# Expert weights of a mixture-of-experts block loaded in transfers of 1 MB on twelve semaphores instead of 2 MB on six

## The chip, the cores and the metric

The kernel runs on one core of a Trainium2 chip. A core has five engines with instruction queues of their own: TensorE (PE, matrix products), VectorE (DVE), ScalarE (ACT), GpSimd (POOL) and SyncE (SP), which here issues most transfers. 16 DMA engines move data between the chip's main memory and the core's on-chip memory of 128 partitions. Engines wait for each other, and for transfers, through semaphores. The metric is the time on the device in microseconds (us); lower is better.

## The reference, cut to what matters

A decoder block: two attention mixers in parallel, then a mixture of experts with 4 of 32 experts for each of 512 tokens, all in float32. The change touches only the expert stage:

```python
D_MODEL = 1024; SEQ = 512; N_EXPERTS = 32; TOP_K = 4; D_FF = D_MODEL
def moe(h, router_w, router_b, w1, b1, w2, b2):
    logits = (xt @ router_w + router_b).astype(jnp.float32)
    top_v, top_i = lax.top_k(logits, TOP_K)
    gate = jax.nn.softmax(top_v, axis=-1)
    ...
    def expert_block(args):
        xb, e = args
        hc = xb @ w1[e] + b1[e]          # w1[e]: 1024 x 2048, 8 MB
        gt = jnp.minimum(hc[:, :D_FF], SWIGLU_LIMIT)
        up = jnp.clip(hc[:, D_FF:], -SWIGLU_LIMIT, SWIGLU_LIMIT)
        glu = gt * jax.nn.sigmoid(SWIGLU_ALPHA * gt)
        return ((up + 1.0) * glu) @ w2[e] + b2[e]   # w2[e]: 1024 x 1024, 4 MB
    ...
```

Each expert has 12 MB of weights, 384 MB in all, and every byte is loaded once.

## The kernel before

**Stages.** Until about 440 us the kernel normalises, projects and runs both attention mixers. From there to about 520 us it forms the output projection, routes the tokens and stores what the experts need. From about 521 us it works through the 32 experts, and at the end it adds up and normalises the rows.

**An expert.** `expert(e, b)` on TensorE (L1729) runs the first product of expert e, `up` (L1670), and then the second product of expert e−1, `second` (L1781), which calls `down` (L1699). `up` takes eight slabs of the first matrix, c = 0 to 7, each 128 partitions of 2048 floats (1 MB), and runs 12 matmuls of 32 x 512 on each (three groups of 32 tokens, four column blocks); the profile counts two records for each of these float32 matmuls, so 24 a slab and 192 an expert. `down` does likewise with four slabs s of the second matrix. Expert 0 is different: `first_expert` (L1745) runs `up` in two rounds, two token groups and then the third, and only the second round reports its slabs as used.

**The ring.** `ring` (L165) holds 12 slabs of 1 MB as six places of two (`pair_slot`, `slab`, L445 and L449). Places 0 and 1 take the second matrix (`W2_SLOTS`), places 4, 5, 2, 3 the first (`W1_LATER`); expert 0 uses places 0 and 1 and four other buffers (`FIRST_SLABS`, L465), loaded by `load_lone` (L672) in single slabs. So all 12 MB of an expert's turn are under way or in use at once.

**Loading.** SyncE issues all of it, in program order. `load_pair(e, u)` (L661) issues one transfer of 2 MB, u = 0 to 3 from the first matrix and 4, 5 from the second; a partition's share is 4096 neighbouring floats. `load_w1(e)` (L713) waits until `w1_used` says that TensorE is through with both slabs of a place, then issues the pair; `load_w2` (L718) does the same with `w2_used`. TensorE counts these up after each slab (`used`). `load_last_w2` (L723) loads expert 31's second matrix into places of the first, in single slabs already, but waits for both slabs of a place. TensorE waits for a pair on `slabs_loaded[u]` ahead of its first slab (L1742, L1788). Each place has a semaphore of its own, since a transfer counts 16 on its semaphore, engine by engine.

**Beside it.** GpSimd gathers each expert's token rows with three indirect transfers (L910) and adds each expert's result into main memory with two (L930, L923), on another queue of the same 16 DMA engines.

Of the kernel before, what the change touches and what calls it, by code (L numbers as in the profile page):

```python
# [146 lines left out]
def hybrid_block(nc, x, positions, norm1_g, w_in, cmp_pos_emb, cmp_w1, cmp_w2, fox_f_bias, w_proj_nsa,  # L147
                 w_proj_fox, w_out, norm2_g, router_w, router_b, expert_w1, expert_b1, expert_w2,
                 expert_b2, norm_f_g, rope_freqs, out):
    with ExitStack() as ctx:  # L150
# [3 lines left out]
        def sem(name):  # L154
            return ctx.enter_context(nc.semaphore(name))
# [294 lines left out]

            return pair_slot(k)[:, 2048 * h:2048 * h + 2048]

        def last_load(s):

            return (last_loaded if s % 2 else slabs_loaded)[s // 2], 16

        def slabs_of(slots):

            return [slab(k, h) for k in slots for h in range(2)]
# [38 lines left out]
        consts2 = sem("consts2")  # L498
        table_stored, last_table_stored = sem("table_stored"), sem("last_table_stored")
        idx_ready = sem("idx_ready")  # L500
        slabs_loaded = [sem("slabs_loaded%d" % b) for b in range(6)]
        w1_used = sem("w1_used")
        w2_used = sem("w2_used")
        now_ready = sem("now_ready")
# [7 lines left out]
        gt_ready = sem("gt_ready")  # L512
        hc_free = sem("hc_free")
        third_root, third_normed = sem("third_root"), sem("third_normed")
        last_loaded = [sem(f"last_loaded{u}") for u in range(2)]
        sg_ready = sem("sg_ready")
        act_ready = sem("act_ready")
        gT_ready = sem("gT_ready")
# [24 lines left out]
        def _(sp):  # L543
# [114 lines left out]
            sp.dma_start(g2k, norm2_g[0].rearrange("(p c) -> p c", p=P)).then_inc(router_loaded, 16)  # L658
            sp.dma_start(r_bias, router_b[0:1, :].partition_broadcast(P)).then_inc(router_loaded, 16)

            def load_pair(e, u):  # L661

                if u < NK // 2:
                    src = expert_w1[0].rearrange("e (p u c) n -> e p u (c n)", p=P, c=2)
                else:
                    src = expert_w2[0].rearrange("e (p u c) n -> e p u (c n)", p=P, c=4)
                at = u % (NK // 2)
                slot = (W1_FIRST if isinstance(e, int) and e == 0 else W1_LATER)[u] if u < NK // 2 else W2_SLOTS[at]
                src = src[bass.ds(e, 1), :, at, :] if not isinstance(e, int) else src[e:e + 1, :, at, :]
                sp.dma_start(pair_slot(slot), src.rearrange("e p n -> (e p) n")).then_inc(slabs_loaded[u], 16)  # L670

            def load_lone(c):  # L672
                src = expert_w1[0].rearrange("e (p c) n -> e p c n", p=P)[0, :, c, :]
# [32 lines left out]
            store_table(EARLY)  # L706
            store_x2(EARLY)
            load_pair(1, 1)
            for u in range(2):
                sp.wait_ge(w1_used, 2 * u + 2)  # L710
                load_pair(0, NK // 2 + u)

            def load_w1(e):  # L713
                for u in range(NK // 2):
                    sp.wait_ge(w1_used, NK * (e - 1) + 2 * u + 2)
                    load_pair(e, u)

            def load_w2(e):  # L718
                for u in range(2):
                    sp.wait_ge(w2_used, 4 * (e - 1) + 2 * u + 2)  # L720
                    load_pair(e, NK // 2 + u)

            def load_last_w2():  # L723
                for s in range(NK // 2):
                    src = expert_w2[0].rearrange("e (p s c) n -> e p s (c n)", p=P, c=2)[E - 1:E, :, s, :]
                    sp.wait_ge(w1_used, NK * (E - 1) + s // 2 * 2 + 2)
                    sp.dma_start(slab(W2_LAST[s // 2], s % 2), src.rearrange("e p n -> (e p) n")).then_inc(*last_load(s))

            load_w1(2)
            load_w2(1)  # L730
# [519 lines left out]
        def _(pe):  # L1250
# [478 lines left out]
            def expert(e, b):  # L1729

                if isinstance(e, int) and e == 1:
                    pe.wait_ge(rows_ready, 1)
                else:
                    pe.wait_ge(hc_free, e)
                def used(c, ins):
                    ins.then_inc(w1_used, 1)
                    if isinstance(e, int) and e == 1 and c == NK // 2:
                        spread_rows(SLOTS_AT, 0, 2 * E, row_of.rearrange("p v e -> p (v e)")).then_inc(table_full, 1)

                pe.wait_ge(xT_ready, e + 2)  # L1740
                up(b, slabs_of(W1_LATER),
                   lambda c: pe.wait_ge(slabs_loaded[c // 2], 16 * e + (16 if c < LONE else 0)) if c % 2 == 0 else None, used)  # L1742
                second(e - 1, 1 - b)

            def first_expert():  # L1745
# [22 lines left out]
                def first_loaded(c):  # L1768
                    if c >= LONE:
                        loaded, value = lone_loaded[c - LONE]  # L1770
                        pe.wait_ge(loaded, value + 16)
                    elif c % 2 == 0:
                        pe.wait_ge(slabs_loaded[c // 2], 16)

                pe.wait_ge(xT_ready, 1)
                up(0, FIRST_SLABS, first_loaded, between,
# [4 lines left out]
            def second(e, b):  # L1781

                pe.wait_ge(gT_ready, e + 1)
                if not (isinstance(e, int) and e == 0):
                    pe.wait_ge(y_ready, e)
                else:
                    pe.wait_ge(idx_ready, 8)
                down(b, W2_SLOTS, lambda s: pe.wait_ge(slabs_loaded[(NK + s) // 2], 16 * e + 16) if s % 2 == 0 else None,  # L1788
                     lambda s, ins: ins.then_inc(w2_used, 1))

            def second_last(b):

                pe.wait_ge(b_last_ready, 2)
                for n, w in enumerate((512, 256)):
                    pe.matmul(ps[:, Y_LAST + n, 0:w], ident[:, :], b_last[n], start=True, stop=False, skip_group_check=True)
                pe.wait_ge(gT_ready, E)
                down_last(b, W2_LAST, lambda s: pe.wait_ge(last_load(s)[0], 16 if s % 2 else 16 * E + 16), lambda s, ins: ins.then_inc(w2_used, 1))

            first_expert()
            expert(1, 1)  # L1800
# [706 lines left out]
```

## Time and profile before

| | us |
|---|---|
| median of 3 runs | 1561.2 (1560.4 to 1562.38) |
| profiled execution | 1560.53 |
| its span | 1558.8 |
| TensorE busy in it | 1513.6 (97%) |
| mean share of the DMA engines' time used by SyncE's queue | 71.2% |
| moved | 463.85 MB |

The span runs from the first to the last instruction of the profiled execution. A busy TensorE is a TensorE with a matmul under way, not one at its peak. TensorE ran at the full granted clock of 2.4 GHz (1.00) throughout the expert loop. In the rows, "DMA share" is the mean busy share of the 16 DMA engines; it can pass 1 where packets overlap. The time of a transfer is given from its issue on SyncE to its landing.

### The profile page before, as it was taken

To read this page: it belongs to the slowest core of one execution; us is meant where nothing else is said; L and a number is where in the kernel's file an instruction comes from. 1 tells how busy PE (TensorE), PEld (TensorE's weight loads), DVE (VectorE), ACT (ScalarE), POOL (GpSimd) and SP (SyncE) were. 2 spreads that over 40 slices of the span, in tenths; PEclk is the share of its full clock that TensorE was granted. 3 is DMA by queue.
4 is the path that set the end of the run, shared out by engine and by line. 5 is a ranking of instruction groups with operands and counts; after the bars stand their busy time and mean duration, and the time that the engine had idled before them with its cause. 6 is when DMAs were issued, how large, how long until landed. Compare 5 with 4: busy or idle time off the path is not lost.

```text
span 1558.8 us, 30600 instructions
## 1 busy us (share of the span) xinstructions
PE 1513.6 (97%) x12626; PEld 625.6 (40%) x12627; DVE 595.9 (38%) x1114; ACT 219.0 (14%) x468; POOL 299.5 (19%) x381
## 2 busy tenths in 40 slices
PE   7999999999999999999999999999999999999993
PEld 4654555666445433333333333333333333333331
DVE  4104555333225562244224433433343334433342
ACT  4212444323212100000000000000000000000001
POOL 2000001533000202122212221222122212121101
PEclk9999999999999999999999999999999999999997
DMA  9122130531273499999999999999999999999984
GB/s 241 28 55 54 41 81 14 167 93 27 71 290 129 172 388 403 415 417 419 414 414 419 419 413 419 417 418 412 419 419 417 411 416 418 415 418 409 412 365 135
DMA packets 109595, 463.85 MB, mean 298 GB/s; under 512 B 33698, under 2 KB 72562, under 8 KB 84464
## 3 DMA queue, kind: packets, MB, share of 16 engines
q1 hardware_dynamic: 95680, 446.42, 71.2%
q0 software_dynamic: 13872, 16.83, 4.7%
q8 instruction: 30, 0.49, 0.1%
q14 instruction: 13, 0.11, 0.0%
HBM read 452.94 MB, written 18.89 MB: 303 GB/s over the span
## 4 chain that ended last, share of the span: by engine, by line
PE 74%; DMA 21%; issue 2%; ACT 1%; DVE 1%; ACTq 0%; DVEq 0%; SPq 0%; PEld 0%; PEldq 0%; POOLq 0%
PE ps L1676 30%; DMA ring<-in_expert_w 20%; PE ps L1260 12%; PE ps L1685 9%; PE ps L1410 7%; PE ps L1694 4%; PE ps L1634 4%; PE ps L1395 2%; PE ps L1372 2%; PE ps L1382 2%; ACT mixT L1091 1%; PE ps L1550 0%; DMA xs<-in_x 0%; PE ps L1586 0%; DMA oT_nsa<-table,v_win 0%
## 5 line engine op out<-in xcount | busy, mean ns | idle before, releaser
L1676 PE MATMUL ps<-ring,oT_fox 128*32 128x512 f32 x6048 | 658.7, 593 | 4.5 <-DMA ring<-in_expert_w 4.0
L1676 PEld LDWEIGHTS ps<-ring,oT_fox 128*32 128x32 f32 x6048 | 194.8, 110 | 447.6 <-issue 410.4
L2332 DVE TENSOR_TENSOR mixT<-ps,mask 128x768 f32<-128x768 f32 x64 | 61.0, 953 | 577.1 <-PE ps L1676 577.1
L1685 PE MATMUL ps<-ring,hT 128*32 128x512 f32 x2048 | 267.8, 592 | 1.5 <-DMA ring<-in_expert_w 1.3
L1694 PE MATMUL ps<-ring,hT 128*32 128x256 f32 x2048 | 158.6, 379 | 0.0
L1410 PE MATMUL ps<-hT,ring 128*128 128x512 f32 x304 | 137.0, 597 | 0.0
L1694 PEld LDWEIGHTS ps<-ring,hT 128*32 128x32 f32 x2048 | 69.3, 110 | 150.0 <-issue 149.9
L910 POOL DMA_INDIRECT oT_nsa<-table,pc x93 | 105.3, 1132 | 47.1 <-POOL pc L905 27.7
L1190 ACT ACTIVATE mixT<-mixT 128x768 f32<-128x768 f32 x32 | 27.0, 844 | 614.6 <-DVE mixT L2336 614.6
L1260 PE MATMUL ps<-hT,ring 128*128 128x512 f32 x208 | 92.1, 603 | 0.2 <-ACT hT L1021 0.2
L1685 PEld LDWEIGHTS ps<-ring,hT 128*32 128x32 f32 x2048 | 68.2, 110 | 59.0 <-issue 17.8
L905 POOL COPY pc<-pc 128x3 int32 (+1 forms) x31 | 7.3, 234 | 406.4 <-DMA x<-hT,v_win 386.1
L1410 PEld LDWEIGHTS ps<-hT,ring 128*128 128x128 f32 x304 | 55.4, 190 | 64.0 <-issue 64.0
L1200 ACT ACTIVATE hT<-rope_pT,v_fox 128x512 f32<-128x512 f32 (+1 forms) x62 | 34.7, 607 | 311.0 <-DVE rope_pT L2368 311.0
L918 POOL COPY v_win<-v_win 128x1 int32 (+1 forms) x64 | 9.7, 178 | 270.8 <-ACT hT L1200 255.1
L930 POOL DMA_INDIRECT x<-hT,v_win x32 | 52.1, 1627 | 43.5 <-POOL v_win L918 25.5
L1091 ACT ACTIVATE mixT<-ps,st 128x128 f32<-128x128 f32 (+1 forms) x96 | 49.1, 535 | 78.5 <-DVE st L1967 78.5
L1260 PEld LDWEIGHTS ps<-hT,ring 128*128 128x128 f32 x208 | 39.7, 193 | 49.0 <-issue 48.8
L1634 PE MATMUL ps<-ring,mixT 128*128 128x512 f32 x128 | 59.4, 602 | 0.0
L2321 DVE STREAM_TRANSPOSE oT_fox<-oT_nsa 128x768 f32<-128x768 f32 x31 | 49.6, 1600 | 7.1 <-DVE mixT L2340 7.1
L923 POOL DMA_INDIRECT x<-hT,v_win x32 | 50.3, 1571 | 9.8 <-issue 9.8
L2328 DVE STREAM_TRANSPOSE hT<-mixT 128x768 f32<-128x768 f32 x32 | 51.2, 1600 | 1.1
(309 smaller groups left out, 1131.7 us busy)
## 6 DMA issues: line engine op xcount, KB each, us to landing
ring<-in_expert_w SPq DMA_DIRECT2D x188, 2048.0 KB, 23.3
ring<-in_w_in SPq DMA_DIRECT2D x28, 512.0 KB, 4.8
ring<-in_w_out SPq DMA_DIRECT2D x8, 512.0 KB, 9.1
ring<-in_expert_w SPq DMA_DIRECT2D x4, 1024.0 KB, 23.6
ring<-in_w_in SPq DMA_DIRECT2D x1, 2144.0 KB, 13.3
xs<-in_x SPq DMA_DIRECT2D x4, 512.0 KB, 5.1
ring<-in_w_in SPq DMA_DIRECT2D x8, 256.0 KB, 3.6
ring<-in_w_proj_nsa SPq DMA_DIRECT2D x16, 128.0 KB, 2.8
```

The source lines that it names most:

```text
L910: pool.indirect_dma_start(out=xg_rows[b][:, 256 * g:256 * g + 256], out_offset=None, in_=table_quarter, in_offset=bass.IndirectOffsetOnAxi ...
L923: pool.indirect_dma_start(out=x2_quarter, out_offset=bass.IndirectOffsetOnAxis(ap=now_quarter[b], axis=0), in_=yb[b][:, 512:768], in_offse ...
L930: pool.indirect_dma_start(out=x2_half, out_offset=bass.IndirectOffsetOnAxis(ap=now_half[b], axis=0), in_=yb[b][:, 0:512], in_offset=None, ...
L1091: last = act.activation(probs[:, h, P_OFF[t]:P_OFF[t] + P * (t + 1)], scores(h, t), ACT.Exp, bias=ngm[:, h, t:t + 1], accum_out=sums[:, h, ...
L1260: last = pe.matmul(dst, lhs(c), rhs(c), start=(c == 0), stop=(c == n - 1))
L1410: ins = pe.matmul(w, w_c(c), hT[:, c, :], start=(c == 0), stop=(c == NK - 1))
L1634: ins = pe.matmul(ps[:, u, :], mix_t[:, t, k, :], w_o[k][:, n * 512:(n + 1) * 512], start=(k == 0), stop=(k == NK - 1))
L1676: ins = pe.matmul(wide(ps[TG * j:TG * j + TG, hc + g, :]), xT[b][:, g, c, :], up_slab(slabs[c], j), start=(c == 0), stop=(c == NK - 1), ti ...
L1685: ins = pe.matmul(ps[TG * q:TG * q + TG, bank, :], gT[b][:, q // 2, c, :], rows[:, at:at + 512], start=(c == 0 and bank == Y_BANK), stop=( ...
L1694: ins = pe.matmul(ps[TG * q:TG * q + TG, bank, 0:256], gT[b][:, 2, c, :], rows[:, at:at + 256], start=(c == 0 and bank == Y_BANK + 1), sto ...
L2328: return dve.transpose(gT[b], act_b.rearrange("p g (m c) -> p g c m", c=NK))
L2332: return dve.tensor_tensor(to, half, b_up[:, 256 * n:256 * n + 256].unsqueeze(1).broadcast_to([P, NG, 256]), ALU.add)
```

## The change

Every transfer of expert weights becomes one slab of 1 MB. `load_slab(e, c)` replaces the body of `load_pair`; a partition's share is now 2048 neighbouring floats. In the loop SyncE waits for one used slab ahead of each transfer. Twelve semaphores take the place of six, and of `last_loaded`; four of them (for the second matrix) are older ones used again, which start from a value that is not zero. TensorE waits ahead of each slab, except in expert 0, where it waits for two slabs ahead of every second one.

```diff
-        slabs_loaded = [sem("slabs_loaded%d" % b) for b in range(6)]
+        slabs_loaded = [(sem("slabs_loaded%d" % c), 0) for c in range(8)]
+        slabs_loaded += [(w_gate_loaded[0], 160), (w_gate_loaded[1], 96), (w_mix_loaded[0], 192), (w_mix_loaded[1], 192)]
...
+            def load_slab(e, c):
+
+                if c < NK:
+                    src = expert_w1[0].rearrange("e (p c) n -> e p c n", p=P)
+                    slabs = slabs_of(W1_LATER) if not (isinstance(e, int) and e == 0) else FIRST_SLABS
+                else:
+                    src = expert_w2[0].rearrange("e (p s c) n -> e p s (c n)", p=P, c=2)
+                    slabs = slabs_of(W2_SLOTS)
+                src = src[bass.ds(e, 1), :, c % NK, :] if not isinstance(e, int) else src[e:e + 1, :, c % NK, :]
+                sp.dma_start(slabs[c % NK], src.rearrange("e p n -> (e p) n")).then_inc(slabs_loaded[c][0], 16)
+
             def load_pair(e, u):
-
-                if u < NK // 2:
-                    src = expert_w1[0].rearrange("e (p u c) n -> e p u (c n)", p=P, c=2)
...
-                sp.dma_start(pair_slot(slot), src.rearrange("e p n -> (e p) n")).then_inc(slabs_loaded[u], 16)
+                for c in (2 * u, 2 * u + 1):
+                    load_slab(e, c)
...
-            for u in range(2):
-                sp.wait_ge(w1_used, 2 * u + 2)
-                load_pair(0, NK // 2 + u)
+            for s in range(4):
+                sp.wait_ge(w1_used, s + 1)
+                load_slab(0, NK + s)
...
             def load_w1(e):
-                for u in range(NK // 2):
-                    sp.wait_ge(w1_used, NK * (e - 1) + 2 * u + 2)
-                    load_pair(e, u)
+                for c in range(NK):
+                    sp.wait_ge(w1_used, NK * (e - 1) + c + 1)
+                    load_slab(e, c)
...
-                    sp.wait_ge(w1_used, NK * (E - 1) + s // 2 * 2 + 2)
-                    sp.dma_start(slab(W2_LAST[s // 2], s % 2), src.rearrange("e p n -> (e p) n")).then_inc(*last_load(s))
+                    sp.wait_ge(w1_used, NK * (E - 1) + s + 1)
+                    sp.dma_start(slab(W2_LAST[s // 2], s % 2), src.rearrange("e p n -> (e p) n")).then_inc(slabs_loaded[s][0], 16)
...
-                   lambda c: pe.wait_ge(slabs_loaded[c // 2], 16 * e + (16 if c < LONE else 0)) if c % 2 == 0 else None, used)
+                   lambda c: pe.wait_ge(slabs_loaded[c][0], 16 * e + (16 if c < LONE else 0)), used)
...
-                down(b, W2_SLOTS, lambda s: pe.wait_ge(slabs_loaded[(NK + s) // 2], 16 * e + 16) if s % 2 == 0 else None,
+                down(b, W2_SLOTS, lambda s: pe.wait_ge(slabs_loaded[NK + s][0], 16 * e + (slabs_loaded[NK + s][1] + 16)),
```

`load_w2` changes as `load_w1` does, and so do the waits of `second_last` and of `first_loaded`.

On SyncE, at the entry to the expert loop (from expert 0's second matrix on), before:

```order
L670 DMA ring<-in_expert_w 128x4096 [waits w1_used] x6
L670 DMA ring<-in_expert_w 128x4096 [waits w2_used] x2
L731 UNCONDITIONAL_BRANCH
L731 ISA
L670 ISA [waits w1_used]
L670 DMA ring<-in_expert_w 128x4096
L715 REGISTER_ALU
```

and now:

```order
L666 DMA ring<-in_expert_w 128x2048 [waits w1_used] x12
L666 DMA ring<-in_expert_w 128x2048 [waits w2_used] x4
L731 UNCONDITIONAL_BRANCH
L731 ISA
L666 ISA [waits w1_used]
L666 DMA ring<-in_expert_w 128x2048
L715 REGISTER_ALU
```

Twice as many transfers of half the size, each behind a wait of its own; nothing else changed its place.

On TensorE, at the end of the first product and the start of the second in the loop, before:

```order
L1676 MATMUL ps<-ring,oT_fox 32x512 [waits slabs_loaded3]
L1676 MATMUL ps<-ring,oT_fox 32x512 x23
L1785 REGISTER_ALU [waits gT_ready]
L1788 ISA [waits y_ready]
L1685 MATMUL ps<-ring,hT 32x512 [waits slabs_loaded4]
L1685 MATMUL ps<-ring,hT 32x512 x3
L1694 MATMUL ps<-ring,hT 32x256 x4
```

and now:

```order
L1676 MATMUL ps<-ring,oT_fox 32x512 [waits slabs_loaded6]
L1676 MATMUL ps<-ring,oT_fox 32x512 x11
L1676 MATMUL ps<-ring,oT_fox 32x512 [waits slabs_loaded7]
L1676 MATMUL ps<-ring,oT_fox 32x512 x11
L1786 REGISTER_ALU [waits gT_ready]
L1789 ISA [waits y_ready]
L1685 MATMUL ps<-ring,hT 32x512 [waits w_gate_loaded0]
L1685 MATMUL ps<-ring,hT 32x512 x3
L1694 MATMUL ps<-ring,hT 32x256 x4
```

The matmuls keep their order; a wait now stands ahead of every 12 of them instead of every 24, and in the second product a register step comes with some of the new waits.

## Rows read from the trace of the kernel before

**Rows 1.** The page: TensorE and DMA engines, busy tenths in 40 slices.
```profile
PE   7999999999999999999999999999999999999993
...
DMA  9122130531273499999999999999999999999984
```

**Rows 2.** The chain that ended last, in order of time: start us, us, what.
```profile
1014.27 20.60 PE ps L1676 x192
1045.19 20.64 PE ps L1676 x192
1065.99 25.69 DMA ring<-in_expert_w
1091.72 5.40 PE ps L1676 x48
...
1474.63 5.36 PE ps L1676 x48
1490.31 20.60 PE ps L1676 x192
```

**Rows 3.** Waits of TensorE's weight loads, 1045 to 1490 us: total, times, longest.
```profile
PEld ps L1676 <- DMA ring<-in_expert_w: 33.2, 51, 1.4
```

**Rows 4.** Transfers issued 612 to 643, then 1091 to 1123 us: KB, us to landing.
```profile
ring<-in_expert_w SPq DMA_DIRECT2D x6, 2048.0 KB, 12.5
...
ring<-in_expert_w SPq DMA_DIRECT2D x6, 2048.0 KB, 25.9
```

**Rows 5.** Timeline of TensorE and of SyncE's issues around 541 and 555 us.
```profile
541.16 1.90 PE L1676 MATMUL ps<-ring,oT_fox 128*32 128x512 f32 x16
542.88 0.50 PE L1661 MATMUL ps<-v_fox,ident 96*32 96x28 f32 x24
...
543.12 2.36 SPq L670 DMA_DIRECT2D ring<-in_expert_w  x2
...
555.46 0.33 SPq L670 DMA_DIRECT2D ring<-in_expert_w  x1
```

**Rows 6.** Busy time by window; the last two columns are DMA share and GB/s.
```profile
540.00:545.00 5.00, 5.00 (x76) 1.71 (x69) 3.19 (x11) 0.00 (x0) 3.28 (x5) 1.00 0.32 60
...
555.00:560.00 5.00, 5.00 (x52) 1.50 (x48) 4.62 (x11) 0.84 (x1) 0.00 (x0) 1.00 0.75 275
560.00:565.00 5.00, 5.00 (x68) 1.71 (x64) 4.67 (x9) 0.00 (x0) 0.00 (x0) 1.00 1.04 413
```

**Rows 7.** DMA queues, 700 to 1000 us: packets, MB, share of 16 engines; issues.
```profile
q1 hardware_dynamic: 8230, 119.84, 94.3%
q0 software_dynamic: 4211, 5.09, 7.1%
...
ring<-in_expert_w SPq DMA_DIRECT2D x59, 2048.0 KB, 19.3
```

**Rows 8.** DMA, 1484 to 1492 us, 16 KB packets.
```profile
DMA packets 240, 3.51 MB, mean 438 GB/s; under 512 B 26, under 2 KB 26, under 8 KB 26
...
q1 hardware_dynamic: 240, 3.51, 102.4%
```

**Rows 9.** DMA, 493 to 496 us, 8 KB packets.
```profile
q1 hardware_dynamic: 171, 1.27, 101.0%
```

**Rows 10.** DMA, 297 to 303 us, 4 KB packets.
```profile
DMA packets 684, 2.49 MB, mean 415 GB/s; under 512 B 77, under 2 KB 77, under 8 KB 683
...
q1 hardware_dynamic: 683, 2.48, 102.1%
```

**Rows 11.** Three issues: start on SyncE, and us to landing.
```profile
441.08 0.43 SPq L670 DMA_DIRECT2D ring<-in_expert_w  x1
...
ring<-in_expert_w SPq DMA_DIRECT2D x1, 2048.0 KB, 8.4
...
442.03 0.43 SPq L674 DMA_DIRECT2D rope_pT<-in_expert_w  x1
...
rope_pT<-in_expert_w SPq DMA_DIRECT2D x1, 1024.0 KB, 12.5
...
443.28 0.59 SPq L670 DMA_DIRECT2D ring<-in_expert_w  x1
...
ring<-in_expert_w SPq DMA_DIRECT2D x1, 2048.0 KB, 21.0
```

**Rows 12.** Lines 1788 and 670: ns min/median/max, first and last start.
```profile
L1788 PEldq FUSED_REGOPS  x14: 37/37/37, 630.3 to 1445.4; - x14
...
L670 SPq DMA_DIRECT2D ring<-in_expert_w x188: 327/333/785, 441.1 to 1490.5; - x188
```

**Rows 13.** The chain of 530 to 562 us: the first expert's second gather.
```profile
533.94 4.44 DMA oT_nsa<-table,v_win
```

More of the change, by code:

```diff
@@ L451, in slab @@
             return pair_slot(k)[:, 2048 * h:2048 * h + 2048]
-        def last_load(s):
-            return (last_loaded if s % 2 else slabs_loaded)[s // 2], 16
         def slabs_of(slots):
@@ L514, in hybrid_block @@
         third_root, third_normed = sem("third_root"), sem("third_normed")
-        last_loaded = [sem(f"last_loaded{u}") for u in range(2)]
         sg_ready = sem("sg_ready")
@@ L659, in _ @@
             sp.dma_start(r_bias, router_b[0:1, :].partition_broadcast(P)).then_inc(router_loaded, 16)
-            def load_pair(e, u):
-                if u < NK // 2:
-                    src = expert_w1[0].rearrange("e (p u c) n -> e p u (c n)", p=P, c=2)
[L665 to L669, printed above, removed]
-                sp.dma_start(pair_slot(slot), src.rearrange("e p n -> (e p) n")).then_inc(slabs_loaded[u], 16)
+            def load_slab(e, c):
[7 more added lines that the diff above has]
+                sp.dma_start(slabs[c % NK], src.rearrange("e p n -> (e p) n")).then_inc(slabs_loaded[c][0], 16)
+            def load_pair(e, u):
+                for c in (2 * u, 2 * u + 1):
+                    load_slab(e, c)
             def load_lone(c):
@@ L708, in _ @@
             load_pair(1, 1)
-            for u in range(2):
-                sp.wait_ge(w1_used, 2 * u + 2)
-                load_pair(0, NK // 2 + u)
+            for s in range(4):
+                sp.wait_ge(w1_used, s + 1)
+                load_slab(0, NK + s)
             def load_w1(e):
-                for u in range(NK // 2):
-                    sp.wait_ge(w1_used, NK * (e - 1) + 2 * u + 2)
-                    load_pair(e, u)
+                for c in range(NK):
+                    sp.wait_ge(w1_used, NK * (e - 1) + c + 1)
+                    load_slab(e, c)
             def load_w2(e):
-                for u in range(2):
-                    sp.wait_ge(w2_used, 4 * (e - 1) + 2 * u + 2)
-                    load_pair(e, NK // 2 + u)
+                for s in range(4):
+                    sp.wait_ge(w2_used, 4 * (e - 1) + s + 1)
+                    load_slab(e, NK + s)
             def load_last_w2():
@@ L1772, in first_loaded @@
                     elif c % 2 == 0:
-                        pe.wait_ge(slabs_loaded[c // 2], 16)
+                        for n in range(2):
+                            pe.wait_ge(slabs_loaded[c + n][0], 16)
                 pe.wait_ge(xT_ready, 1)
@@ L1796, in second_last @@
                 pe.wait_ge(gT_ready, E)
-                down_last(b, W2_LAST, lambda s: pe.wait_ge(last_load(s)[0], 16 if s % 2 else 16 * E + 16), lambda s, ins: ins.then_inc(w2_used, 1))
+                down_last(b, W2_LAST, lambda s: pe.wait_ge(slabs_loaded[s][0], 16 * E + 16), lambda s, ins: ins.then_inc(w2_used, 1))
             first_expert()
```

## The prediction, made before the changed kernel was run

> **What bounds the kernel now.** I read the page by slices first. TensorE is busy almost everywhere, but from the fifteenth slice on the 16 DMA engines are at 9 tenths or more as well [rows 1]. So two resources are full in the expert loop, and the question is which wait ends last. The chain of the work that ended last answers it: until 1045 us an expert's 192 matmuls of the first product follow each other every 30.92 us (1014.27 to 1045.19) with no transfer in the chain; from 1065 us on the chain steps through a weight transfer in nearly every expert [rows 2]. The waits say the same: from 1045 to 1490 us TensorE's weight loads waited 51 times for a transfer of expert weights, 33.2 us in all, which contains 0.3 us each of ordinary spacing [rows 3].
>
> Two periods follow. TensorE alone needs 30.92 us per expert. The transfers need (1474.63 − 1091.72) / 12 = 31.91 us [rows 2], 0.99 us more. Up to 1045 us the difference is paid from the lead of the ring: a transfer lands 12.5 us after its issue in one early expert, 25.9 us after it in a late one [rows 4]. From 1045.19 to 1490.31 us lie 14 experts, 445.12 us, where 14 x 30.92 = 432.88 would do: TensorE loses 12.2 us to transfers. That is all that faster weights could return. The queue never runs dry there, so **issuing a transfer earlier in the middle of the loop brings nothing**. The last binding landing, at 1474.63 us (the fourth pair of expert 30's first matrix), is fixed by when the continuous stretch of DMA work begins and by how much engine time that work takes.
>
> **The change part by part.** *The start of the stretch.* The second matrix of expert 0 is asked for at 543.12 us, when two slabs are used; the 16 matmuls of the first two slabs run from 541.16 us for 1.9 us [rows 5]. The new wait is for one slab, so the request comes one half of 1.72 us earlier (16 matmuls to the next at 542.88), **−0.86 us**. The DMA engines are at 0.32 in that slice [rows 6], so nothing is in the way. The next place comes free at 555.46 us [rows 5]; the engines were at 0.75 between 555 and 560 us and full (1.04) in the slice after it [rows 6]. A half place comes free 2.58 us before (24 matmuls at 0.107 us, a quarter of 20.60 / 2 [rows 2]), while the work before it still runs, so that hole of 0.25 x 5 closes: **−1.25 us**.
>
> *The landing.* Before, TensorE starts a pair when both of its slabs are there. Now it starts the first when that one is there and needs the second 2.58 us later. After the last binding landing one slab, not two, is left of the pair: **−2.58 us**. All three gains together are −4.7 us. With weights of 1 MB the last slabs (expert 31's second matrix) are asked for one slab earlier, which nobody waits for.
>
> *The packets.* A pair row is 4096 floats (16 KB) per partition, a slab row 2048 (8 KB). Each engine moves a slab in eight packets of 8 KB, and moved its share in four of 16 KB. From the first transfer of the stretch to the binding one lie 4 (w2 of expert 0) + 29 x 8 (w1 of 2 to 30) + 28 x 4 (w2 of 1 to 28) = 348 slabs, hence 348 x 4 = **1392 added packets per engine**. What one costs beside its bytes is the decisive unknown. All sizes below include one completion packet to eight data packets, before as after, so nothing more is owed for the doubled completions.
> - 16 KB, in the loop: 8230 packets, 16 x 57 of them completions (59 issues, 119.84 MB is 7314 rows), took 94.3% of 16 x 300 us: 619 ns a row [rows 7]. With hardly any other traffic, 3.51 MB (214 rows) in 102.4% of 16 x 8 us: 612 ns [rows 8].
> - 8 KB: 1.27 MB (155 rows) in 101.0% of 16 x 3 us: 313 ns, or 626 ns for 16 KB [rows 9]. Against 619 and 612 that is **6.7 to 13.1 ns** for the added packet.
> - 4 KB (the output projection's weights): 2.48 MB (606 rows) in 102.1% of 16 x 6 us: 161.7 ns, 647 ns for 16 KB in four packets; three added ones cost 28 to 34.6 ns, **9.4 to 11.5 ns** each [rows 10].
> - By landings, farther off: the one pair lands at 441.08 + 8.4 = 449.5, two 8 KB transfers later it is 442.03 + 12.5 = 454.5, two pairs later 443.28 + 21.0 = 464.3 us [rows 11]. That is 5.05 us against 4.88 for 2 MB: 0.17 us over eight added packets, 21 ns, with an uncertainty of about as much since landings are given to 0.1 us.
>
> The lower end is zero: an engine that reads the next row while it writes the last may show no cost of its own. I see no reason for one below zero. I take 10 ns, where the 4 KB rows stand, which have most packets: 1392 x 10 ns = **+13.9 us**. 6.7 ns gives +9.3, 13.1 gives +18.2.
>
> The Trainium skill ("DMA: Bandwidth & Descriptors", section "Why small descriptors are slow (HBM only)") puts about 3 cycles on each packet, and its section "Where 436 GB/s comes from" gives the fabric 850 MHz; an estimate from these is 3.5 ns, so +4.9 us in place of +13.9, and no change in the sum. The rows of 4 KB packets speak for about three times that.
>
> *Instructions.* TensorE's sequencer gets two or three more register steps per expert in the second product, 37 ns each where such steps stand now [rows 12]. Now they stand between the products, and the pass still takes 30.92 us, so they hide behind queued matmuls. Uncovered, three per expert would be 0.11 us, less than the 0.99 us by which transfers are the longer, so even then nothing. SyncE issues 12 transfers per expert and not 6, about 0.33 us each [rows 12]: 4 us of 31. *Expert 0's second gather* (4.44 us on the chain [rows 13]) shares engines with long packets; shorter ones could bring it forward by a few tenths, counted at nothing.
>
> Sum: 13.9 − 4.7 = +9.2 us. The profiled execution took 1560.5 us (span 1558.8 and 1.7 around it), 0.7 below the median of 1561.2: **1570.4 us** on the median.
>
> **The rivals.** *Overhead overlaps.* An added packet costs nothing because the next row's read is under way, and only the three gains are left: 1561.2 − 4.7 = **1556.5 us**, faster. It decides from 3.4 ns (4.7 / 1392) down. For it: packets overlap in the records, whose shares exceed 100% [rows 8, 10]. Against: shares exceed it for 4 KB packets too, and these move 415 GB/s where the 16 KB ones move 438 in their window. *A small overhead*, 1.2 to 5.6 ns, leaves the sum within 3.1 us of nothing; at 3.5 ns it is 1561.2 + 0.2 = **1561.4 us**. This is the result the section on small descriptors would give, and the rows lie above it. *A cost per transfer*, not per packet, as the landings would have it at 21 ns per packet: 28.7 − 4.7 gives **1585 us**; the windows of packets, which are finer, speak against it. That the lead is not gained (the binding wait moves on to expert 30's second matrix) would change the sum by under 2.6 us and lies inside the range.
>
> **How the numbers follow.** The likeliest case, 5.7 to 13 ns, holds 0.68 and gives 1564.5 to 1575. Small overhead 0.14, overlap 0.13, cost per transfer 0.05. A measurement of this kernel tells about 0.2%, 3.1 us, from no change. Slower is 0.68 + 0.05 less what of the first could still measure as the same: 0.71; same 0.16; faster 0.13. The range goes from 1556 (all overlapped) to 1577, which takes in 13.1 ns and some 2 us more; what it leaves out is most of the cost-per-transfer case and the tails, under 0.2.
>
> **What would show it.** Right, if the period of binding landings late in the loop is about 31.91 + 48 x 0.010 = 32.4 us, an 8 KB packet in the loop takes half of 629 ns, the first wait of TensorE for a transfer comes earlier than 1065 us, and the request for expert 0's second matrix starts near 542.3. The three gains are right if the hole at 555 to 560 us is gone and waits end with one slab of 24 matmuls before the next landing. I am wrong if the period stays at 31.9 us, which means no cost per packet; or if gathers and scatters, now served between shorter packets, take less engine time than the 7.1% they have [rows 7], which I counted as unchanged.

## The result and the profile after

| | before | after |
|---|---|---|
| median | 1560.8 (1559.86 to 1562.38, 6 runs) | 1569.82 (1568.09 to 1572.27, 6 runs) |
| span of the profiled execution | 1558.8 | 1566.3 |
| ratio | | 1.0055 [1.0045, 1.0065] |

The change makes the kernel slower by 9.0 us, where 9.2 was forecast. Both kernels' slices look alike at first, and that is the first reading: nothing new stands still, the same resource is full for longer. The page after, TensorE's and the DMA engines' busy tenths in 40 slices (they answer [rows 1]), then queue q1 over the whole span (packets, MB, share of 16 engines):

```profile
PE   7999999999999999999999999999999999999993
...
DMA  9122130521283599999999999999999999999994
...
q1 hardware_dynamic: 122752, 446.43, 72.0%
```

The chain of work that ended last, of after (start, duration, what; it answers [rows 2]):

```profile
982.75 20.60 PE ps L1676 x192
1013.67 12.87 PE ps L1676 x120
1026.58 2.78 PE ps L1676 x24
1029.40 5.87 PE ps L1676 x48
1035.43 29.00 DMA ring<-in_expert_w
...
1485.18 28.03 DMA ring<-in_expert_w
1513.26 5.41 PE ps L1676 x48
```

Until 1013.67 us TensorE keeps its 30.92 us per expert, as before. The first wait for weights comes inside that expert, at 1026.6 us, and not behind 1045.19: the ring's lead is used up one expert sooner. The last piece is new too. Before, the last binding landing was at 1474.63 us in expert 30 and TensorE ran at its own pace from there. Now it is the landing at 1513.26 us, in expert 31's first matrix, with two slabs (48 matmuls) left.

**The start of the stretch.** Timeline of after (start, us; [rows 5] is the same place before):

```profile
540.29 1.90 PE L1676 MATMUL ps<-ring,oT_fox 128*32 128x512 f32 x16
...
541.39 1.19 SPq L666 DMA_DIRECT2D ring<-in_expert_w  x2
```

The request starts 1.10 us after the 16 matmuls do, and started 1.96 us after them: 0.86 us earlier, the first term of the sum. The matmuls themselves also start 0.87 us earlier (540.29 against 541.16). That isn't the change's doing: SyncE's first issue into the ring is already 0.9 us earlier (440.2 us, [rows 12] has 441.1), and the granted clock of the first 100 us was 1.00 in this execution and 0.98 in the one of before. Then the windows of after (TensorE, weight loads, DVE, ACT, POOL busy; granted clock; DMA share; GB/s; before in [rows 6]):

```profile
540.00:545.00 5.00, 5.00 (x72) 1.55 (x60) 1.44 (x7) 0.00 (x0) 3.54 (x5) 1.00 0.58 196
545.00:550.00 5.00, 4.85 (x69) 2.68 (x69) 3.50 (x9) 0.00 (x0) 0.22 (x1) 1.00 1.01 402
550.00:555.00 5.00, 5.00 (x52) 1.45 (x48) 4.66 (x11) 0.00 (x0) 0.00 (x0) 1.00 0.96 375
555.00:560.00 5.00, 5.00 (x52) 1.56 (x48) 4.65 (x10) 0.84 (x1) 0.00 (x0) 1.00 1.05 357
```

From 555 to 560 us the DMA engines are full (1.05) where they were at 0.75. The hole is closed.

**In the loop.** DMA, 700 to 1000 us, of after ([rows 7] before):

```profile
DMA packets 20440, 123.18 MB, mean 411 GB/s; under 512 B 4097, under 2 KB 4241, under 8 KB 5999
...
q1 hardware_dynamic: 16244, 118.31, 95.0%
q0 software_dynamic: 4196, 4.88, 7.0%
...
x<-hT,v_win POOLq DMA_INDIRECT x20, 9.4
```

118.31 MB are 14442 rows of 8192 bytes, which took 95.0% of 16 x 300 us: 315.8 ns each, 631.5 for 16 KB where one 16 KB row took 619. The added packet costs 12.6 ns by the rows. Queue q0, GpSimd's gathers and scatters, keeps its share (7.0%, before 7.1%), but a scatter lands 9.4 us after its issue instead of 13.1.

TensorE's waits of 900 to 1500 us, after (us in all, times, longest):

```profile
PEld ps L1676 <- DMA ring<-in_expert_w: 61.0, 106, 1.5
PEld ps L1685 <- DMA ring<-in_expert_w: 26.2, 52, 1.1
```

Before, the first of these rows had 51 waits in the same stretch, the numbers of [rows 3]. There are twice as many now and they are a little shorter, 0.58 us each instead of 0.65, since TensorE goes on at each slab.

### The profile page after: what moved, and what is told of

It is laid out like the page before. It is cut to its first block, busy times and chain, and to the rows that moved or that the text cites. A ratio compares the mean times of both kernels' runs of the same rounds, so it can differ in the third digit from the quotient of the medians.

```text
span 1566.3 us, 31381 instructions
## 1 busy us (share of the span) xinstructions
PE 1517.4 (97%) x12626; PEld 616.5 (39%) x12627; DVE 594.7 (38%) x1114; ACT 219.1 (14%) x468; POOL 290.7 (19%) x381
## 4 chain that ended last, share of the span: by engine, by line
PE 70%; DMA 19%; SPq 5%; issue 2%; DVE 1%; ACT 1%; ACTq 0%; DVEq 0%; PEld 0%; PEldq 0%; POOLq 0%
PE ps L1676 27%; DMA ring<-in_expert_w 18%; PE ps L1260 12%; PE ps L1685 9%; PE ps L1410 7%; SPq L666 5%; PE ps L1694 4%; PE ps L1634 4%; PE ps L1395 2%; PE ps L1372 2%; PE ps L1382 2%; ACT mixT L1091 1%; PE ps L1550 0%; DMA xs<-in_x 0%; PE ps L1586 0%
## 5 line engine op out<-in xcount | busy, mean ns | idle before, releaser
L1694 PEld LDWEIGHTS ps<-ring,hT 128*32 128x32 f32 x2048 | 66.6, 110 | 152.7 <-issue 152.6
L910 POOL DMA_INDIRECT oT_nsa<-table,pc x93 | 97.2, 1045 | 47.1 <-POOL pc L905 26.9
L1685 PEld LDWEIGHTS ps<-ring,hT 128*32 128x32 f32 x2048 | 63.5, 110 | 69.8 <-DMA ring<-in_expert_w 26.2
## 6 DMA issues: line engine op xcount, KB each, us to landing
ring<-in_w_in SPq DMA_DIRECT2D x1, 2144.0 KB, 13.1
```

The lines of the kernel that those rows point to most:

```text
L910: pool.indirect_dma_start(out=xg_rows[b][:, 256 * g:256 * g + 256], out_offset=None, in_=table_quarter, in_offset=bass.IndirectOffsetOnAxi ...
L1685: ins = pe.matmul(ps[TG * q:TG * q + TG, bank, :], gT[b][:, q // 2, c, :], rows[:, at:at + 512], start=(c == 0 and bank == Y_BANK), stop=( ...
L1694: ins = pe.matmul(ps[TG * q:TG * q + TG, bank, 0:256], gT[b][:, 2, c, :], rows[:, at:at + 256], start=(c == 0 and bank == Y_BANK + 1), sto ...
```

## The experiments

Three theories stood against each other. **Per packet**: each added packet costs its engine some 10 ns, and the half-sized release and wait give back 4.7 us. **Per transfer**: it is the doubled number of transfers that costs. **Small overhead**: packets cost next to nothing. Ratios are against the kernel before on the same chip.

### Halves alone

Transfers of 1 MB, but released and awaited in pairs as before. Against after:

```diff
                 for c in range(NK):
-                    sp.wait_ge(w1_used, NK * (e - 1) + c + 1)
+                    if c % 2 == 0:
+                        sp.wait_ge(w1_used, NK * (e - 1) + c + 2)
                     load_slab(e, c)
...
-                   lambda c: pe.wait_ge(slabs_loaded[c][0], 16 * e + (16 if c < LONE else 0)), used)
+                   lambda c: [pe.wait_ge(slabs_loaded[c + n][0], 16 * e + (16 if c < LONE else 0)) for n in range(2)] if c % 2 == 0 else None, used)
```

The second matrix likewise.

> Transfers of 1 MB in pairs: both slabs of a place are asked for together once both are used, and TensorE waits for both ahead of the first. So this has the smaller transfers without the earlier release and without the wait per slab. If 1392 added packets at 10 ns each cost 13.9 us and the two kinds of finer waiting gave back 4.7 us in the changed kernel, this is 1560.8 + 13.9 = about 1575 us, ratio to before 1.009. Rival: the finer waits give nothing, and the packets cost only what was measured for the whole, 9 us: then this is 1570 us, ratio 1.0058, as the changed kernel is.

Measured: 1575.37 us against 1560.44, ratio 1.0095 [1.0078, 1.0112]. 14.9 us over 1392 added packets per engine are 10.7 ns each. The hole is back, in the windows of this kernel (columns as above), here with the matmuls of the first two slabs, the first request behind them (SyncE's timeline, 538 to 580 us), and the last landing that TensorE waited for, from the chain:

```profile
540.00:545.00 5.00, 4.25 (x24) 1.74 (x28) 2.16 (x10) 0.00 (x0) 3.38 (x5) 0.67 0.17 47
555.00:560.00 5.00, 5.00 (x52) 1.47 (x48) 4.72 (x9) 0.00 (x0) 0.00 (x0) 1.00 0.72 297
...
545.13 1.89 PE L1679 MATMUL ps<-ring,oT_fox 128*32 128x512 f32 x16
...
547.09 28.84 SPq L666 DMA_DIRECT2D ring<-in_expert_w  x12
...
1522.86 5.36 PE ps L1679 x48
```

The stretch begins 4.0 us later here than before (547.09 against 543.12), so the hole does too: it lies between 558 and 562 us, with DMA shares of 0.54, 0.06, 0.79 and 0.79 in slices of one us. This profiled execution is the slowest of its kernel (1577.67 us). TensorE stood idle for 1.1 us around 540 us, waiting for a gather, and then had a granted clock of 0.50, the lower level (1.2 GHz), from 542 to 545 us. The two executions above show 1.00 there. How early an execution reaches the stretch varies, from 539 to 545 us for these matmuls over the profiles of this document, and that is in every end-to-end number below.

So the change is a cost of about 15 us and a gain of about 6 (1.0095 against 1.0055 is 6.2 us, the medians' differences 14.9 and 9.0 give 5.9; forecast 4.7). The traces, with the different starts taken out, give the 4.7 us that were forecast: expert 31's first product ends at 1522.86 + 5.36 = 1528.22 us here and at 1513.26 + 5.41 = 1518.67 us in after, 9.55 us apart, and 4.84 of these are the start (545.13 against 540.29).

### 2 MB in rows of 8 KB

Before, with the number of transfers left alone: one transfer of 2 MB whose two slabs are not neighbours in main memory, so a partition gets two rows of 8 KB. TensorE takes the slabs in the order 0, 4, 1, 5 and so on.

```diff
+                    slot, rows = (W1_FIRST if first else W1_LATER)[u], slice(2 * u, 2 * u + 2) if first else slice(u, u + NK // 2 + 1, NK // 2)
...
-                sp.dma_start(pair_slot(slot), src.rearrange("e p n -> (e p) n")).then_inc(slabs_loaded[u], 16)
+                to = ring[:, 2 * slot:2 * slot + 2, :]
+                sp.dma_start(to, src.rearrange("e p c n -> (e p) c n")).then_inc(slabs_loaded[u], 16)
```

> Transfers of 2 MB as before, waits by place as before, but a place holds two slabs that do not lie beside each other in main memory (u and u+4), so each partition's share is two rows of 8 KB and not one of 16 KB. The products take the slabs in the order in which they lie in the ring. Cost per packet: as p1, about 1575 us, ratio 1.009. Cost per transfer (completions, issues, SyncE held up): as before, 1561 us, ratio 1.000. It also tells what holds up SyncE's issues: number of transfers under way (then issues stay at 0.33 us) or number of packets (then issues of some us as in the changed kernel).

Measured: 1573.27 us, ratio 1.0087 [1.007, 1.0103]. 12.8 us come with the small packets although not one transfer was added: 9.2 ns a packet. The first request (SyncE's timeline, 538 to 580 us) and the last binding landing:

```profile
541.00 39.51 SPq L673 DMA_DIRECT2D ring<-in_expert_w  x8
...
1516.96 5.36 PE ps L1683 x48
```

What the halves alone cost beyond that, 2.1 us at the medians for 188 more transfers, lies inside the two intervals. Per packet is right, per transfer is at most a small rest.

### Rows of 4 KB

The pair as two transfers of 1 MB, each with half of every slab's columns, so all rows are 4 KB. Released and awaited in pairs. Against before:

```diff
-                sp.dma_start(pair_slot(slot), src.rearrange("e p n -> (e p) n")).then_inc(slabs_loaded[u], 16)
+                src = src.rearrange("e p (k h n) -> (e p) h k n", k=2, h=2)
+                to = pair_slot(slot).rearrange("p (k h n) -> p h k n", k=2, h=2)
+                sp.dma_start(to[:, 0, :, :], src[:, 0, :, :]).then_inc(slabs_loaded[u], 16)
+                sp.dma_start(to[:, 1, :, :], src[:, 1, :, :]).then_inc(other_loaded[u][0], 16)
```

> Two transfers of 1 MB for each place as in p1, with waits by place, but each transfer takes half of the columns of both slabs, so packets are of 4 KB. Cost per packet at 10 ns: 12 added packets for each of 348 slabs and engine, 4176 x 10 ns = 41.8 us, about 1603 us, ratio 1.027. Cost per transfer: the same as p1, 1575 us, ratio 1.009.

Measured: 1601.49 us, ratio 1.026 [1.0243, 1.0278]. 41.0 us over 3 x 1392 = 4176 added packets are 9.8 ns each; three times the packets cost about three times as much (41.0 against 14.9 and 12.8 us). The DMA rows of this kernel, 1100 to 1400 us:

```profile
q1 hardware_dynamic: 29722, 114.58, 96.2%
...
x<-hT,v_win POOLq DMA_INDIRECT x18, 8.0
...
545.99 0.37 SPq L674 DMA_DIRECT2D ring<-in_expert_w  x1
...
1547.55 5.36 PE ps L1681 x48
```

114.58 MB are 27974 rows of 4 KB at 165.1 ns, or 660 ns for 16 KB. (The last two lines are again the first request and the last binding landing.) In this kernel the chain runs over SyncE's issues for 44% of the span; they take 2.1 and 2.2 us at the median, up to 5.6. The DMA engines are full all the same, with a share of 1.03 from 1100 to 1400 us, so the trace shows no idle time of theirs that late issues could have caused.

The Trainium skill ("DMA: Bandwidth & Descriptors", section "Why small descriptors are slow (HBM only)") puts about 3 cycles on a packet, an estimate of 3.5 ns at the 850 MHz of its section "Where 436 GB/s comes from". The three runs measure 9.2 to 10.7 ns end to end, and 8.6 to 8.8 ns along their chains (below), two and a half to three times that; the measurement decides.

### Half the partitions in each transfer, twice

A 16 KB row per partition as before, but two transfers of 1 MB per pair: lower and upper 64 partitions in the first of these kernels, even and odd ones in the second. Here packets stay and transfers double.

```diff
-                sp.dma_start(pair_slot(slot), src.rearrange("e p n -> (e p) n")).then_inc(slabs_loaded[u], 16)
+                src, to = src.rearrange("e p n -> (e p) n"), pair_slot(slot)
+                sp.dma_start(to[0:64, :], src[0:64, :]).then_inc(slabs_loaded[u], 16)
+                sp.dma_start(to[64:128, :], src[64:128, :]).then_inc(other_loaded[u][0], 16)
```

The second kernel has `to[0:P:2, :]` and `to[1:P:2, :]`.

> Two transfers of 1 MB for each place, waits by place, but each transfer takes half of the partitions, so that packets stay at 16 KB. Cost per packet: as before within 2 us, ratio 1.000. Cost per transfer: 1575 us, ratio 1.009. If engines are loaded unevenly by half the partitions this may come out slower for a third reason; the mean time of a packet in the loop then stays at 619 ns while the busy share of the engines falls.

Measured: 2316.37 us, ratio 1.4847 [1.4811, 1.4884], far outside every theory. Its DMA row, then its window, 1100 to 1400 us:

```profile
q1 hardware_dynamic: 4945, 64.85, 96.8%
...
1100.00:1400.00 300.00, 203.32 (x1644) 63.06 (x1640) 65.07 (x79) 9.81 (x15) 34.12 (x40) 0.85 1.01 225
```

The engines are busy the whole time (share 1.01) and move 225 GB/s, where they moved 416: 64.85 MB are 3958 rows of 16 KB at 1.17 us. The granted clock of TensorE, which now waited for weights, averaged 0.85. So this run says nothing about transfers, and the next one was made to find the reason.

> As p6 (two transfers of 1 MB for a place, 16 KB packets, waits by place), but the first takes the even and the second the odd partitions, where p6 took the lower and the upper 64. If p6 was slow (2316 us, a 16 KB row at 1.17 us) because a transfer to 64 neighbouring partitions loads only half of the paths into the on-chip memory, this one loads all and comes near before: 1561 to 1564 us (188 added transfers at the 11 ns or so each that p1 less p4 shows: 2 us). If it was slow because a transfer of 64 partitions as such runs at half the rate, this is 2316 us again.

Measured: 1562.12 us against 1560.8, ratio 1.0012 [1.0002, 1.0022]. Its DMA rows of the same stretch:

```profile
DMA packets 13165, 124.90 MB, mean 416 GB/s; under 512 B 3975, under 2 KB 4079, under 8 KB 5857
...
q1 hardware_dynamic: 9133, 119.74, 94.5%
```

Same sizes, same count of transfers, full rate: the halved rate is that of 64 neighbouring partitions, although the transfer behind it in the queue went to the other 64. Now the question on transfers is settled as well: 188 added ones with the data packets unchanged cost 1.3 us (1.9 by the ratio), about a tenth of what after's packets cost. By the trace it is less still: the first request comes at 542.07 us and the last binding landing at 1473.91 us, 0.3 us more between them than before, for 174 added transfers. The Trainium skill ("SBUF — State Buffer", section "Door 1: The DMA port swizzle (why `[64,N]` ≈ `[32,N]`)") says that 64 neighbouring partitions reach 8 of the 16 ports of the on-chip memory, and by its table every second partition reaches all 16; the trace agrees for both kernels, with 225 and 416 GB/s.

### The two halves of the gain, one at a time

After, with only the release by slab (TensorE waits for pairs), and after, with only the wait by slab (SyncE waits for pairs). Each takes one of the two edits of the first experiment. The first:

```diff
-                   lambda c: pe.wait_ge(slabs_loaded[c][0], 16 * e + (16 if c < LONE else 0)), used)
+                   lambda c: [pe.wait_ge(slabs_loaded[c + n][0], 16 * e + (16 if c < LONE else 0)) for n in range(2)] if c % 2 == 0 else None, used)
```

and the second:

```diff
-                    sp.wait_ge(w1_used, NK * (e - 1) + c + 1)
+                    if c % 2 == 0:
+                        sp.wait_ge(w1_used, NK * (e - 1) + c + 2)
```

> Transfers of 1 MB, each asked for as soon as its slab is used, but TensorE waits for both slabs of a place ahead of the first (the earlier start alone, without the wait per slab). By the prediction's terms the earlier start is worth 2.1 us (0.86 for the first request, 1.25 for the hole at 555 to 560 us): 1575.4 - 2.1 = 1573.3 us, ratio to before 1.0083. Rival: the finer waits work only together and this equals the kernel with neither, 1575.4 us, ratio 1.0095.

> Transfers of 1 MB asked for in pairs once both slabs of a place are used, but TensorE waits slab by slab. The prediction gives this 2.58 us, one slab less behind the last binding landing: 1575.4 - 2.6 = 1572.8 us, ratio 1.0079. Rival: as above, 1575.4 us, ratio 1.0095.

Measured: 1572.54 us, ratio 1.0067 [1.0052, 1.0083], and 1572.36 us, ratio 1.0067 [1.0052, 1.0082]. Beside the halves alone (1.0095) each gives back 4.4 us by the ratios, 2.8 and 3.0 by the medians; 2.1 and 2.6 were forecast. The intervals overlap that of the halves alone by a little, so by the times the sign is likely and the size isn't settled. The traces say more. From the first two slabs' matmuls to the end of expert 31's first product, the kernel with the earlier release needs 2.1 us less than the halves alone (545.22 to 1520.84 + 5.36 = 1526.20 us), as forecast. From the first request on, the kernel with the wait by slab needs 3.7 us less (544.46 to 1516.52 + 5.41 = 1521.93 us), 1.1 more than forecast. Both gains together are about what after has, by the medians (2.8 + 3.0 against 5.9).

### Small at the ends, large in between

If packets cost and half places gain only where the stretch begins and where the last landing binds, then slabs belong there alone. The first matrices of experts 2 to 4, 30 and 31 and the second matrices of 0 to 3 and 29 to 31 are loaded and released by slab, the others in pairs of 16 KB rows. The main part of the code, against after:

```diff
+        PHASES = [(3, 5, 1), (5, 29, 2), (29, 30, 2), (30, 31, 1), (31, 32, 1)]
...
+            def load_expert(e, n):
+                for c in range(0, NK, n):
+                    sp.wait_ge(w1_used, NK * e + c + n)
+                    load_rows(e + 1, c, n)
+                for c in range(0, NK // 2, n):
+                    sp.wait_ge(w2_used, 4 * (e - 1) + c + n)
+                    load_rows(e, NK + c, n)
```

(First expert, end, slabs per transfer.)

> 1 MB transfers with waits by slab only where the prediction says that they bring something: the second matrices of experts 0 to 3 and 29 to 31 and the first matrices of 2 to 4, 30 and 31; all others 2 MB as before. The gains of 4.7 us stay, and of the 1392 added packets about 260 stay, 2.6 us at 10 ns: 1560.4 - 4.7 + 2.6 = 1558.3 us, ratio 0.9987, the same as before or just under. Rival (the small transfers were needed throughout to keep the gains, or a hole opens where the kind changes): 1561 us or more.

Measured: 1558.24 us against 1561.32, ratio 0.9978 [0.997, 0.9987]: 3.1 us faster than before, where 2.1 were forecast, and 11.6 faster than after, measured in another round (12.0 by the ratios). The chain of this kernel:

```profile
1152.25 5.40 PE ps L1720 x48
1157.81 26.01 DMA ring<-in_expert_w
...
1487.37 20.60 PE ps L1720 x192
```

The first landing that binds comes behind 1152 us, where it was past 1045 before and at 1026 in after. 1.5 us of that lead is only this execution's: its matmuls of the first two slabs start at 539.71 us, before's at 541.16. The rows of 16 KB take 620 ns here (8219 packets, 94.4%, 1100 to 1400 us):

```profile
q1 hardware_dynamic: 8219, 119.74, 94.4%
...
PEld ps L1720 <- DMA ring<-in_expert_w: 25.6, 38, 1.4
```

### Larger still: 32 KB, and what it broke

The same with four slabs in one transfer for experts 9 to 28 (`(5, 9, 2), (9, 29, 4)` in the table above): half the packets of before.

> As p7, but from expert 9 to 28 the weights come in transfers of 4 MB with 32 KB of one row to a partition. If the cost per packet holds between 16 and 32 KB, 20 experts x 12 slabs x 2 packets fewer = 480 packets per engine give back 4.8 us at 10 ns: 1558.3 - 4.8 = 1553.5 us, ratio 0.9955. Rivals: the overhead ends at 16 KB (a 32 KB row is cut or costs the same per byte) and it equals p7, 1558.3 us; or the release of four slabs at a time lets the queue run dry, and it is slower than before, above 1563 us, with the busy share of the DMA engines below 1 in the middle of the loop.

Measured: 1580.57 us, ratio 1.0118 [1.0095, 1.0141]. The forecast failed in sign. In the trace TensorE no longer waits for weights at all. The chain of 790 to 950 us runs over GpSimd's scatters:

```profile
803.59 27.20 DMA x<-hT,v_win
...
839.44 30.20 DMA x<-hT,v_win
...
877.95 29.58 DMA x<-hT,v_win
...
916.58 23.18 DMA x<-hT,v_win
```

and the waits (600 to 1500 us) and DMA rows (1100 to 1400 us) of this kernel say the same:

```profile
POOL pc L949 <- DMA x<-hT,v_win: 560.6, 27, 29.0
...
PE ps L1720 <- DVE oT_fox L2372: 22.5, 4, 6.4
...
q1 hardware_dynamic: 3902, 113.71, 89.5%
...
x<-hT,v_win POOLq DMA_INDIRECT x20, 19.7
```

From one scatter in the chain to the next lie 35.9, 38.5 and 38.6 us, more than the 30.92 of an expert on TensorE. GpSimd doesn't gather the next tokens before its last scatter has landed, so TensorE waits for tokens. The DMA engines, at a share of 0.96 in this stretch, are no longer what binds. And nothing was won in return: 113.71 MB are 3470 rows of 32 KB at 1238 ns, 619 ns for 16 KB, as before.

Two things differ from the run before it, packets of 32 KB, and places released and awaited by fours. The last kernel keeps the fours and goes back to 16 KB rows:

```diff
-                    load_rows(e + 1, c, n)
+                    for at in range(c, c + n, min(n, 2)):
+                        load_rows(e + 1, at, min(n, 2))
```

> As p8 (four slabs asked for together and waited for together from expert 9 to 28), but each group of four as two transfers of 2 MB with 16 KB packets. If the 32 KB packets made p8 slow, by holding up the small packets of gathers and scatters (scatters took 19.7 us in p8, 13.1 with 16 KB, 9.3 with 8 KB packets), this is as p7, 1558 us, up to 1561, with scatters back at 13 us. If the coarse release and the coarse wait made it slow, it is about 1580 us like p8, with the DMA engines' share below 1 in the middle of the loop.

Measured: 1562.62 us against 1560.8, ratio 1.0002 [0.9992, 1.0011]. Scatters land after 12.8 us again and TensorE's weights bind:

```profile
x<-hT,v_win POOLq DMA_INDIRECT x18, 12.8
```

Of the 22 us that were lost against pairs between the ends, the 32 KB packets account for 18 (1.0118 against 1.0002) and the coarse release and wait for 4 (1.0002 against 0.9978).

## Why the prediction was right, step by step

**Which resource binds** held. A TensorE that waits only behind 1045 us, and DMA engines full from 560 us on, meant that engine time is what counts; every run that changed engine time per byte moved the end by it.

**The packets.** 10 ns was taken, from [rows 10], with 6.7 and 13.1 as ends. Measured end to end: 10.7 (halves alone), 9.2 (2 MB in 8 KB rows) and 9.8 ns (4 KB). These hold the varying start, and count only the packets up to expert 30. The time from the first request to the last binding landing doesn't. Before, it runs from 543.12 to 1474.63 us; at the same pace of 31.91 us an expert's worth of slabs later is 1506.54 us, and 11 slabs later 1503.88. Against that, shifted by each kernel's own first request:

| kernel | first request, us | last binding landing, us | late by, us | added packets | ns each |
|---|---|---|---|---|---|
| halves alone | 547.09 | 1522.86 | 12.4 | 1440 | 8.6 |
| 2 MB in 8 KB rows | 541.00 | 1516.96 | 12.5 | 1440 | 8.7 |
| rows of 4 KB | 545.99 | 1547.55 | 38.1 | 4320 | 8.8 |
| after (1.25 us of hole closed) | 541.39 | 1513.26 | 12.4 | 1436 | 8.6 |

The kernel with the wait by slab alone gives 7.9 ns, that with the earlier release alone 8.6. So the term was right in kind and about a seventh too large. The direct reading of rows in the loop gives more: 12.6 ns for 8 KB, and (660 − 620) / 3 = 13.4 for 4 KB. An 8 KB row takes 315.8 ns, half of 631.5 where 629 was forecast. This reading overstates, since packets overlap: the window's DMA share rose from 1.01 to 1.02 with it.

```profile
1100.00:1400.00 300.00, 293.83 (x2996) 92.86 (x2988) 114.90 (x137) 18.52 (x28) 61.59 (x72) 1.00 1.02 410
```

The bytes moved don't depend on that. From 700 to 1000 us they are 119.84 MB before and 118.31 after, one 16 KB share of an engine in 656.2 and in 664.7 ns: 8.5 ns for the added packet. What within a packet takes this time no run separates. From 16 to 32 KB it isn't seen at all (620 and 619 ns), so a fixed cost of every packet is shown from 4 to 16 KB only.

**The period.** 32.4 us per expert was forecast for the binding landings. After's chain has a landing at the same slab (48 matmuls left) six experts ahead of the last:

```profile
1319.53 6.26 PE ps L1676 x48
```

That is (1513.26 − 1319.53) / 6 = 32.29 us, and 31.91 before: 0.38 more, 0.48 were expected. The direction is right, the size is at 7.9 ns a packet.

**The sum along the chain.** Slab 6 of expert 31 lands at 1513.26 us, 9.4 us behind before's pace (1503.88). The stretch began 1.73 us earlier, 0.86 by the change and 0.87 because this execution was early, and the hole gave 1.25, so the 1436 added packets cost 12.4 us, where 13.9 were put down. From that landing on, 5.41 us of matmuls are left and end at 1518.67. Before, the same product ended at 1490.31 + 20.60 = 1510.91. The 7.8 us between them are the 7.5 us by which the two profiled spans differ; the medians differ by 9.0.

**The gains.** The earlier request (0.86 us) is there to the letter, and the hole is closed. What the prediction had wrong here is where the last binding landing lies. It took it to stay in expert 30. The stream is later and slower, so expert 31's first matrix binds as well, and the wait by slab gives less than 2.58 us. With pairs at before's pace this product would end at 1506.54 + 5.36 = 1511.90 us, 1.0 behind before's 1510.91, and with slabs at 1503.88 + 5.41 = 1509.29, 1.6 ahead. So the landing brought 1.6 us, not 2.6. In all: 12.36 − 0.86 − 1.25 − 1.62 = 8.6 us, and the early start of this execution makes 7.8 of it. The packets were taken 1.5 us too dear and the landing 1.0 us too generous. The two errors have opposite signs and both are small, so the hit to 0.2 us on the medians is partly luck; the sign and the size within a microsecond or two are not.

**Counted at nothing.** TensorE's register steps: until 1013.67 us the pass takes 30.92 us as before, so they are hidden. The gathers and scatters did keep their engine share, which was the condition named. That they land 2.2 to 3.7 us sooner (13.1 and 9.4 us from 700 to 1000 us, 11.5 and 9.3 from 1100 to 1400) brought nothing here, since GpSimd isn't on the chain; the run with 32 KB packets shows that it can be. Expert 0's second gather cost nothing in after (TensorE was idle for under 0.2 us ahead of the stretch, as before). It can cost more than the tenths that were thought of: in the profiled executions of the halves alone and of the 4 KB rows TensorE waited 1.1 and 2.7 us for it.

**Wrong without a consequence.** The prediction put SyncE's issues at 0.33 us each. All issues of line 666 in after (ns min/median/max, first and last start):

```profile
L666 SPq DMA_DIRECT2D ring<-in_expert_w x376: 327/1384/3947, 440.2 to 1497.5; - x188
```

The median is 1.38 us, the longest 3.9, where [rows 12] had 333 ns and 785. Twelve of them per expert are 17 us of 32, half of SyncE's time. The issues also stand in the chain of after, with 5 percent of the span (by line, on its page):

```profile
PE ps L1676 27%; DMA ring<-in_expert_w 18%; PE ps L1260 12%; PE ps L1685 9%; PE ps L1410 7%; SPq L666 5%; PE ps L1694 4%; PE ps L1634 4%; PE ps L1395 2%; PE ps L1372 2%; PE ps L1382 2%; ACT mixT L1091 1%; PE ps L1550 0%; DMA xs<-in_x 0%; PE ps L1586 0%
```

A late issue would cost something only if the DMA engines ran dry, and they are full (1.02) in the loop. The 2 MB transfers in 8 KB rows are the stronger argument: none of their issues took over 0.8 us, and they cost 8.7 ns a packet all the same. The halves alone have as many transfers as after, issues of 0.33 us at the median, and 8.6 ns a packet:

```profile
L666 SPq DMA_DIRECT2D ring<-in_expert_w x376: 190/333/1470, 442.5 to 1507.7; - x188
```

So the issues aren't the price of the change.

**The rivals.** Overlap (1556.5) is excluded by every run with small packets, small overhead (1561.4) by the ratio's lower end of 1.0045 and by the 8.6 ns, cost per transfer (1585) by the 2 MB transfers in 8 KB rows and by the even and odd partitions. (Its price has a slip that changes nothing: 1392 x 21 ns are 29.2 us, not 28.7.)

## What to carry to other kernels

Where the DMA engines are full, count packets as well as bytes: at 8 KB and 4 KB each cost about 9 ns beside its data, and from 16 to 32 KB nothing was left to win. When two kernels differ by a few microseconds, take out of the traces how early each of them reached the changed part; here that alone moved by up to 6 us. A finer release pays only where the queue runs dry and behind the last landing that binds, so use small transfers there and large ones between. Then look who else uses these engines: the row size of the large stream sets how long the small indirect transfers take, and past some size they become the bound.

## What the hardware showed beyond that

- A scatter from GpSimd beside a saturated stream landed after 8.0, 9.4, 11.2 to 13.1 and 19.7 us with stream packets of 4, 8, 16 and 32 KB, at an unchanged share of the engines of about 7%.
- 16 KB took 660, 632, 620 and 619 ns in the loop as rows of 4, 8, 16 and 32 KB.
- Transfers to 64 neighbouring partitions ran at 225 GB/s even though the next one in the queue went to the other 64; to every second partition they ran at 416.
- SyncE's issue of a 1 MB transfer took 0.33 us or up to 3.9 us. In the kernel with 2 MB transfers of the same packets it stayed under a microsecond:

```profile
L673 SPq DMA_DIRECT2D ring<-in_expert_w x188: 430/543/804, 439.0 to 1501.2; - x188
```

With transfers of 1 MB in rows of 16 KB (even and odd partitions) they stayed short as well; here those of the even half, while the odd half's had a longest of 1.2 us:

```profile
L673 SPq DMA_DIRECT2D ring<-in_expert_w x188: 471/475/798, 440.1 to 1489.8; - x188
```

Small packets and the doubled count of transfers together aren't enough either. The halves alone have both and stay at 0.33 us (longest 1.5), and so does the kernel with the earlier release alone (longest 1.7). With the wait by slab alone the longest is 3.7, and with rows of 4 KB the median is over 2 us. What is exhausted then stays open.
